# Turned one-hots and token weights ahead of the key rows in the expert-picking stage of a transformer layer

## What is computed

```python
def peer_ffn(h, w_q, sub_keys_1, sub_keys_2, expert_u, expert_v):
    ...
    v1, i1 = lax.top_k(s1, PEER_TOPK)
    v2, i2 = lax.top_k(s2, PEER_TOPK)
    cand = (v1[..., :, None] + v2[..., None, :]).reshape(B, S, PEER_HEADS, PEER_TOPK * PEER_TOPK)
    cidx = (i1[..., :, None] * N_KEYS + i2[..., None, :]).reshape(B, S, PEER_HEADS, PEER_TOPK * PEER_TOPK)
    top, pos = lax.top_k(cand, PEER_TOPK)
    eidx = jnp.take_along_axis(cidx, pos, axis=-1)
    gate = jax.nn.softmax(top, axis=-1)
    ...
    def block(args):
        h_t, idx, g = args
        u = jnp.take(expert_u, idx, axis=0)
        act = jax.nn.gelu(jnp.einsum('td,tkd->tk', h_t, u), approximate=False)
        vv = jnp.take(expert_v, idx, axis=0)
        return jnp.einsum('tk,tkd->td', g * act, vv)
```

## Time and profile before

| what | us |
|---|---|
| median of 3 runs | 1944.31 |
| lowest and highest | 1942.71 to 1945.88 |
| the profiled execution | 1944.77 |
| its span, first to last instruction | 1943.0 |
| PE (TensorE) busy | 1844.7 (95%) |
| DVE (VectorE) busy | 1318.0 (68%) |
| ACT (ScalarE) busy | 389.4 (20%) |
| POOL busy | 801.7 (41%) |

### The profile page before, as it was taken

The page is one execution under the profiler, slowest core; times in us unless marked ns, Lnnn a source line. Parts: engine busy times, 40 slices in busy tenths (PEclk is TensorE's granted clock), DMA queues, the critical chain, the costliest instruction groups (busy, mean ns, idle before and its releaser), DMA issues.

```text
span 1943.0 us, 28027 instructions
## 1 busy us (share of the span) xinstructions
PE 1844.7 (95%) x10737; PEld 1427.3 (73%) x10737; DVE 1318.0 (68%) x2611; ACT 389.4 (20%) x842; POOL 801.7 (41%) x789
## 2 busy tenths in 40 slices
PE   3899999999998999999999999888989999999998
PEld 3787788777874458888888888777876666556664
DVE  5855666656665022598999975699986666666665
ACT  3022222222221021011111111488740000000001
POOL 2002212122112000355444444337888888744583
PEclk8789999999999999999999999999999999999999
DMA  9957656865565655889999999877439999999996
GB/s 396 420 192 269 252 189 221 307 241 223 198 261 239 259 167 209 329 320 408 404 406 409 406 409 409 327 229 210 146 124 409 409 408 409 409 408 409 409 408 281
DMA packets 124380, 609.06 MB, mean 313 GB/s; under 512 B 15584, under 2 KB 15712, under 8 KB 101216
## 3 DMA queue, kind: packets, MB, share of 16 engines
q1 hardware_dynamic: 66496, 330.33, 43.9%
q0 software_dynamic: 57344, 274.76, 37.0%
q10 hardware_dynamic: 416, 2.25, 0.3%
HBM read 603.09 MB, written 4.19 MB: 313 GB/s over the span
## 4 chain that ended last, share of the span: by engine, by line
PE 79%; DVE 8%; DMA 8%; issue 2%; POOL 2%; ACT 1%; DVEq 0%; SPq 0%; ACTq 0%
PE ps L1397 22%; PE ps L1314 20%; PE ps L989 13%; PE ps L1037 6%; PE ps L1223 6%; DMA arena<-in_v_dense 3%; PE ps L1074 3%; DMA arena<-in_ada 2%; PE ps L1369 2%; DVE arena L1458 2%; DVE ps L1778 2%; DVE arena L1770 2%; DMA arena<-in_w_in 1%; POOL arena L610 1%; PE ps L1340 1%
## 5 line engine op out<-in xcount | busy, mean ns | idle before, releaser
L1397 PE MATMUL ps<-arena 128*128 128x368 f32 x1536 | 477.3, 473 | 7.0 <-DMA arena<-in_v_dense 6.3
L1397 PEld LDWEIGHTS ps<-arena 128*128 128x128 f32 x1536 | 300.7, 196 | 182.3 <-DMA arena<-in_v_dense 10.9
L1839 DVE SCALAR_TENSOR_TENSOR arena<-arena 128x944 f32<-128x944 f32 x254 | 305.1, 1201 | 172.1 <-DMA arena<-in_v_rows,arena 171.1
L594 POOL DMA_INDIRECT arena<-in_u_rows,arena x256 | 259.9, 1015 | 344.4 <-DVE arena L1770 283.8
L594 POOL DMA_INDIRECT arena<-in_v_rows,arena x256 | 340.2, 1329 | 136.9 <-DVE arena L1839 83.7
L1314 PE MATMUL ps<-arena 128*128 128x256 f32 x1792 | 386.9, 379 | 0.0
L1314 PEld LDWEIGHTS ps<-arena 128*128 128x128 f32 x1792 | 340.4, 190 | 46.2
L989 PE MATMUL ps<-arena 128*128 128x256 f32 x1440 | 350.1, 386 | 1.8 <-DMA arena<-in_w_in 1.8
L1770 DVE SCALAR_TENSOR_TENSOR arena<-arena,ps 128x1152 f32<-128x1152 f32 x208 | 277.4, 1348 | 51.5 <-DMA arena<-in_u_rows,arena 51.3
L989 PEld LDWEIGHTS ps<-arena 128*128 128x128 f32 x1440 | 261.1, 190 | 40.1 <-DMA arena<-in_w_in 3.4
L1437 DVE SCALAR_TENSOR_TENSOR arena<-arena 128x2048 f32<-128x2048 f32 x60 | 143.5, 2392 | 4.6 <-DMA arena<-in_ada 4.6
(11 more groups left out here) (251 smaller groups left out, 1766.3 us busy)
## 6 DMA issues: line engine op xcount, KB each, us to landing
arena<-in_ada SPq DMA_DIRECT2D x96, 1024.0 KB, 7.1
arena<-in_v_dense SPq DMA_DIRECT2D x128, 552.0 KB, 8.4
arena<-in_u_dense SPq DMA_DIRECT2D x128, 448.0 KB, 7.0
arena<-in_w_in SPq DMA_DIRECT2D x45, 1024.0 KB, 7.6
arena<-in_w_tail SPq DMA_DIRECT2D x32, 1024.0 KB, 8.4
arena<-in_w_in SPq DMA_DIRECT2D x12, 512.0 KB, 16.6
arena<-in_u_rows,arena POOLq DMA_INDIRECT x256, 10.0
arena<-in_v_rows,arena POOLq DMA_INDIRECT x256, 11.1
```

Source lines behind the costliest of these rows:

```text
L594: nc.gpsimd.indirect_dma_start(out=row, out_offset=None, in_=table[:, :], in_offset=bass.IndirectOffsetOnAxis(ap=i32(idx[:, b, k:k + 1]), ...
L1397: last = mm(sums(b)[:, g, :], dense[:, b, j // 2, :, j % 2], w[:, g * VG:(g + 1) * VG], start=(j == 0), stop=(j == NKEYS - 1))
L1839: stt(total[b], row, w, total[b], ALU.mult, ALU.add).then_inc(v_sum, 1)
```

## The change

On TensorE the order inside an iteration is altered: the turn of the one-hot and the token weights stand ahead of the key rows. Three waits go with it. TensorE waits for the finished one-hot ahead of the turn. ScalarE, which makes a one-hot into the buffer used two groups before, now waits for the key rows of that group, since they are its last reader. And ScalarE's copy of the turned one-hot waits for the key rows of its own group too, since it is written over the table that they read.

```diff
@@ one_hot(q)
                 if q >= 2:
-                    act.wait_ge(turned, q - 1)
+                    act.wait_ge(y_ps, q - 1)
@@ keep_turned(q)
                 act.wait_ge(turned, q + 1)
+                act.wait_ge(y_ps, q + 1)
@@ TensorE's loop
             for q in range(T // 4):
                 if q + 1 < T // 4:
                     spread_keys(q + 1)
+                pe.wait_ge(hot_out, 2 * q + 2)
+                turn_one_hot(q)
+                if q >= P // 4 + LAG:
+                    token_weights(q - P // 4 - LAG)
                 key_rows(q)
-                turn_one_hot(q)
                 if q == P // 4:
                     turn_products(0)
                 if q == P // 4 + 2:
                     turn_weights(0)
-                if q >= P // 4 + LAG:
-                    token_weights(q - P // 4 - LAG)
```

## The result

| | us |
|---|---|
| before, median of 4 runs | 1944.3 (1942.71 to 1945.88) |
| changed kernel, median of 4 runs | 2039.12 (2034.88 to 2045.19) |
| ratio, with 95% interval | 1.0488 (1.0475 to 1.05) |
| profiled execution of the changed kernel | 2037.34, span 2035.6 |

The change costs 95 us. The forecast was 2011.5, with a range up to 2036: the sign and most of the size were right, and the time lies just outside the range, on the side of the first rival. The spread of the four runs is new too: 10 us, against 3 before.

A forecast was written before the change was run, and what follows sets the result against it. VectorE was taken to bound the 157.6 us expert-picking stage. Terms 0.4 + 6.2 + 1.4 + 60.2 - 1 = +67.2 us on the profiled 1944.8 gave 2012.0, forecast as a 2011.5 us median; range 2002 to 2036.

The forecast's parts named there:

- the first rival: Last 27 groups: TensorE's clock falls; every second group 2035 us, all 2061; 22% for part of the groups, 3% for all.
- VectorE bounds the stage and never waits; key rows made ahead are what keeps it so: Expert-picking stage, 157.6 us: VectorE sets its time; TensorE's order is free while VectorE always finds key rows ready.
- The ring in the last 27 groups: VectorE's picks to weighting, TensorE's token weights, then key rows wait in turn: 5.11 us a group, +60.2 us.
- The smaller ring of 2.36 us: First 32 groups: key rows, ScalarE's copy and turn wait in turn, 2.36 us a group: 75.5 against 69.34, +6.2 us.
- The waits that were to show it: First 32 groups: VectorE waits about 1.3 us at each of six groups without a dot.
- The four groups between: Groups between the first 32 and last 27: gelu and weight turning lengthen them to 11.8 us from 10.40, +1.4.
- +0.4 for the first turn: Start of the first 32 groups: the very first key rows stand behind a turn, +0.4 us.
- -1 behind the loop: Leftover token weights behind the loop: TensorE reaches the first group after 3.01 us instead of 3.23, -1 us.
- VectorE's weightings gain little from POOL being elsewhere: Last 27 groups: two weightings take 0.59 us beside POOL's products, 0.55 without; 1 us could return, left out.
- The 22 us: Last 27 groups: by the exclusive-lock rule, 0.82 us a group could be won back, sum 1990; the prediction rejected it.
- The second rival: Last 27 groups: the ring does not close, TensorE and ScalarE set 3.41 us a group; 1966 us, 6%.
- the 1.84 taken: Last 27 groups: token weights and key rows together cost 1.84 us more in a group caught at low clock.

The follow-up runs named there:

- experiment 2: Kernel before, with only the token weights moved ahead of the key rows and the turn left behind them: 2034.71 us, ratio 1.045.
- experiment 4: Changed kernel, with VectorE making its weighted one-hots one group earlier: 1962.19 us, ratio 1.0089 to the kernel before.
- 7: Kernel before in its own order, plus a TensorE wait for VectorE's weighting ahead of the key rows in the last 27 groups: 1982.57 us, ratio 1.0189.
- Experiment 8: Kernel before, with 13 unread matmuls in TensorE's two idle spells behind the loop: 1942.74 us against 1945.3, ratio 0.9986.
- experiment 3: Changed kernel, with six unread matmuls in TensorE's wait in each of the last 27 groups: 2012.05 us, ratio 1.0343 to the kernel before.
- 1: Changed kernel with the token weights put back behind the key rows, so only the turn is moved: 1952.37 us, ratio 1.0039 to the kernel before.

## Why the prediction was right, and where it was wrong

- *VectorE bounds the stage and never waits; key rows made ahead are what keeps it so.* Right. Its instructions in the last 27 groups are unchanged, and its waits are the loss.
- *The ring in the last 27 groups: 3.01 + 0.89 + 1.21 = 5.11 us, 138.0 in all.* Right at full clock: 5.13, and 138.44 with fillers. Experiments 2, 4 and 7 show that it is this ring: it comes with the token weights alone, it opens when the weights are a group older, and without the products in it a group takes 4.22.
- *The smaller ring of 2.36 us, 75.5 us for 32 groups.* Right: 75.52, and 75.44 with the turn alone moved. That it fits to the hundredth is luck: turn to key rows took 0.38 where the sum had 0.44, and key rows to the copy 1.27 where it had 1.21. The waits that were to show it, 1.3 us at each of the six groups without a dot, came out smaller: none behind the first of them, 0.73 behind the second, 1.14 behind the other four. VectorE has 0.9 us of other work in each of groups 2 and 4, which the prediction's pace of 2.35 left out; it runs late by that and makes it up at the groups without a dot. In a stretch that the ring paces this costs nothing.
- *The four groups between, 11.8 us.* 11.70.
- *+0.4 for the first turn.* Cannot be told: the first picks began at 1243.03 in the changed kernel and 1243.82 before, and at 1243.2 to 1245.7 in the eight experiments; the stages ahead scatter by more.
- *-1 behind the loop.* From the last picks' begin to the dense sums, 1494.05 to 1540.24, makes 46.2 us against 46.5, so -0.3. The first leftover group did come 3.02 us behind the picks (1497.07), as forecast. The clock fell there in the changed kernel too (0.93 in its row). Experiment 8 shows what that fall is worth, 2 us.
- *VectorE's weightings gain little from POOL being elsewhere.* Right. Two take 0.61 at 1450.32, with POOL's products over a microsecond later, and took 0.59 beside them. Only in the last four groups did they take 0.78 to 0.82 before, beside POOL's products, against 0.60 now, less than 1 us in all. The 22 us that the Trainium skill's rule of an exclusive lock ("SBUF — State Buffer", section "Who interferes with whom") would have given back do not exist here.
- *The second rival* (ring not closed, 1966 us) was wrong for the change, but its ring is real: experiment 4 opened the other one and took 1962.19, at 3.35 us a group where the rival had 3.41.

**The step that failed** is the weighing of the first rival: "a slow group makes TensorE busier, which should bring the clock back", with 22% for falls in part of the groups and a range that ended at 13 of them. Fourteen groups ran at half clock in a row, with TensorE busy for 72.89 of 96.01 us, and the clock did not come back between them. In the thirteen behind them TensorE was less busy, 39.16 of 67.79 us, and the clock was at 0.96: it came up at about 1428, was down once more from about 1435 to 1438.5, and then stayed up for 58 us. So the forecast put the fall at nothing, and experiment 3, where it doesn't happen, takes the forecast's time. The price of a slow group was nearly right: 1.73 us (6.86 less 5.13) against the 1.84 taken. 14 x 1.73 = 24.2, and 1.2 for one group of 6.32 makes 25.4; the sum of 2012.0 for the profiled execution plus 25.4 is 2037.4, measured 2037.34. That it lies only just outside the range is luck too: the range ended at every second group, 13 of them, and what came was 14 in a row. Which groups fell in the other three executions is not known, as they have no trace.

The Trainium skill ("TensorE: Matmul & The Clock Gate", section "HAM oscillation — how this bites in real kernels") lays such falls to idle gaps longer than any of this ring. The trace disagrees: the longest wait of TensorE's loads in each slow group was 1.55 us, and 2.02 in the first of them, where the clock fell; in the groups at full clock near the end that wait was longer, 1.83 to 1.85. So the length of the wait alone doesn't tell the two apart. The prediction kept that rule from deciding, but leaned to its side in the chances. The rows at 1400 to 1406, with TensorE busy for 2.46 of 4 us ahead of the fall, were the better witness: that is a fall in this very code, behind a TensorE that works and waits by turns as in the new ring.

Why the level holds for 14 groups in one execution, and in another (experiment 2) alternates for 21 groups and then holds for six, stays open. That it differs from one execution to the next is the likely source of the spread of the times, 10 us here against 2 to 4 us in the experiments whose traces have the clock up nearly throughout (1, 3, 4, 7), but it isn't shown. The mean granted clocks of the four executions don't settle it: the slowest, 2045.19 us, had 0.967, and the profiled one, 2037.34, had 0.962. As experiment 2 shows, what a fall costs depends also on whether TensorE has work in it.

## What to carry to other kernels

When a product is moved ahead of another on an in-order engine, ask what it waits for, and whether the engine that must make that is itself fed by what now stands behind it: the ring's time is the sum round it, and could be had here from the rows before the change to 0.02 us (5.11 against 5.13). One group more of lead for VectorE opened this one. A ring also leaves TensorE idle for a part of each turn, so price its half clock as a likely case, not a remote one. A few unread matmuls in the wait are a quick test of it, and here were a gain: 27 us with six a group.

## What was not expected of the hardware

- The granted clock stayed at either level with the same instructions a group: at 0.50 for 95 us (about 1333 to 1428), and at 1.00 for 58 us (1438.5 to 1496.5), with one short spell of each between.
- In the profiled execution of experiment 2 the clock alternated, full while TensorE mostly waited (0.95 busy of 3.40 us) and half while it worked (3.40 of 3.40). A group so caught took up to 6.77 us, nearly the 6.86 of one at half clock throughout.
- Adding 162 unread matmuls (324 instructions) to TensorE took 27 us off the changed kernel, and 13 (26 instructions) took 2.6 us off the kernel before.
